# A two-layer block on one core: how the first layer's pool stage applies its modulation, and what the first expert weights wait for

## The reference, cut to what matters

```
sh1, sc1, g1, sh2, sc2, g2 = silu(c) @ w_mod[0] + b_mod[0]       # 6 x 1024, once for c and once for c_ctx
a = rmsnorm(x) * norm1_g * (1 + sc1) + sh1                        # per channel
mean_g = windowed mean over tokens of a (windows 2, 4, 8, 16, one per group of 256 channels)
y = ((mean_g - a) @ pool_w[g] + pool_b[g]) * pool_ls
x = x + g1 * y
h = rmsnorm(x) * norm2_g * (1 + sc2) + sh2
gates = top 2 of 16 experts in the best group, from h @ w_route   # hierarchical
x = x + g2 * sum_e gates[e] * (silu(h @ w_gate[e]) * (h @ w_up[e])) @ w_down[e]
```

## Time and profile before

| | |
|---|---|
| median of three runs | 2296.31 us |
| the profiled execution | 2297.54 us, of which span 2296.1 us |
| PE busy | 2149.3 us, 94% |
| DVE, ACT, POOL busy | 1295.4, 1033.7, 134.8 us |
| head and route, to the last store's landing | 0 to 137.4 us |
| first layer's experts | 142.7 to 322.7 us |
| DMA over the span | 324.17 MB, mean 141 GB/s |

### The profile page before, as it was taken

One profiled execution on the slowest core, in us unless ns is written; L12 is line 12 of the kernel. 1 busy time (PEld: TensorE's weight loads), 2 busy tenths in 40 slices (PEclk: granted clock), 3 DMA queues, 4 the chain that ended last, 5 costly groups with the idle time before them and its releaser, 6 DMA issues.

```text
span 2296.1 us, 31361 instructions
## 1 busy us (share of the span) xinstructions
PE 2149.3 (94%) x13248; PEld 1648.1 (72%) x13248; DVE 1295.4 (56%) x1837; ACT 1033.7 (45%) x1501; POOL 134.8 (6%) x112
## 2 busy tenths in 40 slices
PE   6879989999996998999889999998999998999997
PEld 4666654577774665777667888886877776888885
DVE  2467766666637775355526766535255546766533
ACT  3446632155535664377745433324333355433331
POOL 0011200000001220000001000003000002000000
PEclk9979999999997998999999999999999999999998
DMA  9889980022217995211012222121322112212210
GB/s 400 325 344 368 382 348 0 1 111 94 93 47 276 352 361 219 83 65 38 37 74 92 91 110 110 74 100 61 109 94 79 63 56 91 111 74 110 110 55 37
DMA packets 40574, 324.17 MB, mean 141 GB/s; under 512 B 7231, under 2 KB 8255, under 8 KB 21695
## 3 DMA queue, kind: packets, MB, share of 16 engines
q1 hardware_dynamic: 27288, 288.91, 32.6%
q0 software_dynamic: 10624, 25.71, 3.3%
q10 hardware_dynamic: 2512, 7.41, 0.8%
HBM read 310.40 MB, written 24.19 MB: 146 GB/s over the span
## 4 chain that ended last, share of the span: by engine, by line
PE 85%; DVE 6%; ACT 4%; DMA 3%; issue 1%; POOL 0%; SPq 0%; ACTq 0%; POOLq 0%; DVEq 0%
PE PS L163 79%; PE PS L911 2%; DMA work<-tokens,slots 1%; PE PS L661 1%; DVE work L2360 1%; ACT work L1606 1%; PE PS L1172 1%; DVE WR L2366 1%; DMA tokens<-work 0%; ACT XH L1304 0%; ACT work L1611 0%; ACT L1611 0%; DMA work<-ys 0%; DMA work<-in_xtok 0%; ACT work L1602 0%
## 5 line engine op out<-in xcount | busy, mean ns | idle before, releaser
L163 PE MATMUL PS<-HS,RS 128*128 128x512 f32 x4128 | 951.2, 391 | 9.4 <-DVE HS L2137 8.6
L163 PEld LDWEIGHTS PS<-HS,RS 128*128 128x128 f32 x4128 | 773.8, 188 | 175.5 <-issue 13.9
L1780 DVE TENSOR_TENSOR RS<-ring,RS 128x1024 fp32r<-128x1024 f32 x212 | 259.0, 1225 | 342.3 <-ACT RS L1268 342.3
L1268 ACT ACTIVATE RS<-ring 128x1024 fp32r<-128x1024 f32 x212 | 221.6, 1052 | 252.3 <-PE PS L163 252.3
L1703 ACT ACTIVATE work<-work,vec 128x512 f32<-128x512 f32 x88 | 72.0, 818 | 239.5 <-DVE work L2487 239.5
L1780 DVE TENSOR_TENSOR CR<-ring,WR 128x1024 fp32r<-128x1024 f32 x128 | 153.3, 1221 | 35.9 <-ACT WR L1268 33.2
L163 PE MATMUL PS<-work 128*64 128x128 f32 (+5 forms) x1728 | 131.2, 293 | 29.6 <-DVE work L1839 19.7
L1268 ACT ACTIVATE WR<-ring 128x1024 fp32r<-128x1024 f32 x128 | 134.8, 1058 | 50.7 <-PE PS L163 46.9
L163 PEld LDWEIGHTS PS<-work 128*64 128x64 f32 (+2 forms) x1728 | 106.9, 147 | 49.3 <-issue 30.9
L1268 ACT ACTIVATE work<-PS 128x384 f32<-128x384 f32 (+2 forms) x194 | 86.9, 484 | 115.8 <-PE PS L694 37.4
L163 PE MATMUL PS<-RS,HS 128*128 128x512 f32 x480 | 116.1, 400 | 8.3 <-DVE HS L2137 8.3
(11 more groups left out here) (258 smaller groups left out, 2804.8 us busy)
## 6 DMA issues: line engine op xcount, KB each, us to landing
ring<-in_wexp SPq DMA_DIRECT2D x32, 2048.0 KB, 11.1
ring<-in_wmod SPq DMA_DIRECT2D x24, 2048.0 KB, 10.2
ring<-in_ffnu SPq DMA_DIRECT2D x22, 2048.0 KB, 8.0
ring<-in_wexp SPq DMA_DIRECT2D x32, 1024.0 KB, 11.2
ring<-in_ffnd SPq DMA_DIRECT2D x10, 2048.0 KB, 7.3
ring<-in_dilqk SPq DMA_DIRECT2D x6, 2048.0 KB, 8.1
ring<-in_sbqk SPq DMA_DIRECT2D x4, 2048.0 KB, 8.1
ring<-in_dilv SPq DMA_DIRECT2D x3, 2048.0 KB, 8.0
```

Source lines behind the costliest of these rows:

```text
L163: return T.matmul(out, l, r, start=start, stop=stop, skip_group_check=True)
L1268: return S.activation(out, x, ACT.Copy, **kw)
L1780: V.tensor_tensor(lo, src, hi.bitcast(F32), ALU.subtract).then_inc(w_lo, 1)
```

## The change

The head applies the first modulation to the copied means instead of to the weights. DVE's `scaled_means(s)` multiplies the 8 chunks of a stream in place by `aff`; `shift_edges(s)` adds sh1 times the edge constants straight to the first and last 8 tokens of `HT` and signals `ad_aff`. So `shift_products` and `add_edges` go, one `poolw` serves both streams, `product(i)` waits for `ad_aff` 3 (latent) or 4 (context), and the ring's cell 8 is free. Because sh1 is needed before the products, modulation tiles 2 and 3 are turned ahead of them. On PE, `rows(6)` moves in front of the latent sums and the context sums stand behind `stat_spread(2)`. On ACT, the last four products stand between the first four squares. SP waits for all token stores before `wup` 0 and for the first gather before `wup` 1.

```diff
@@ the ring, and the products on PE
-    ring.over[8] = (pl_y, 17)
...
             def product(i):
                 s, c = i // 8, i % 8
-                g = c // 2
                 pe.wait_ge(*(means_copied(12 + i) if i < 4 else (md_b, i - 3)))
-                pe.wait_ge(md_a, 8 * s + 2 * g + 2)
+                pe.wait_ge(ld_work, 16)
+                pe.wait_ge(ad_aff, s + 3)
...
-            def shift_products():
...
@@ order on PE, from cols(1) on
+            rows(2)
+            rows(3)
+            cols(2)
+            cols(3)
             for i in range(4):
                 product(i)
...
@@ ACT
-            for i in range(16):
+            ada(2, 6)
+            ada(3, 7)
+            for i in range(12):
                 product(i)
-                if i % 4 == 3:
-                    ada(2 + i // 4, 6 + i // 4 % 2)
+                if i in (3, 7):
+                    ada(4 + i // 4, 6 + i // 4)
             for c in range(8):
                 square(2, c, XL[:, c, :], pl_x, c + 1)
+                if c < 4:
+                    product(12 + c)
+            ada(6, 6)
             root(2)
-            ada(6, 6)
+            ada(7, 7)
@@ DVE
-            def scaled_weights(s):
+            def scaled_means(s):
+                dve.wait_ge(pl_ma, 4 * s + 4)
+                dve.wait_ge(pl_md, 4 * s + 4)
                 for c in range(8):
-                    V.tensor_scalar(scaled_w[s][:, c // 2, c % 2, :], poolw[:, c // 2, c % 2, :], aff[:, 0, 0, c, s:s + 1],
-                                    None, ALU.mult).then_inc(md_a, 1)
+                    x = pool_rows(8 * s + c)
+                    V.tensor_scalar(x, x, aff[:, 0, 0, c, s:s + 1], None, ALU.mult).then_inc(md_a, 1)
...
+                dve.wait_ge(md_a, 8 * s + 8)
+                V.tensor_tensor(h[:, :, 0:8], h[:, :, 0:8], e[:, :, 0:8], ALU.add)
+                V.tensor_tensor(h[:, :, n - 8:n], h[:, :, n - 8:n], e[:, :, 8:16], ALU.add).then_inc(ad_aff, 1)
...
             ada(2, 6)
             ada(3, 7)
-            dve.wait_ge(pl_y, 13)
-            for s in range(2):
-                shift_edges(s)
-            add_edges(0)
+            dve.wait_ge(ad_mod, 4)
+            shift_edges(0)
+            scaled_means(1)
+            shift_edges(1)
@@ SP
         for n in range(6, 16):
             load("wmod", n)
+        sp.wait_ge(ht_out, 96)
         load("wup", 0)
+        sp.wait_ge(xg[0], 16)
         load("wup", 1)
```

More of the change, by code:

```diff
@@ L554, in pool_mix @@
             cols(1)
+            rows(2)
+            rows(3)
+            cols(2)
+            cols(3)
             for i in range(4):
                 product(i)
-            rows(2)
+            rows(4)
             product(4)
             product(5)
-            cols(2)
+            cols(4)
             product(6)
             product(7)
-            rows(3)
+            rows(5)
             product(8)
             product(9)
[L566 to L576, removed]
             cols(5)
+            for i in range(10, 16):
+                product(i)
+            rows(6)
             for c in range(8):
                 stat_add(2, c)
-            rows(6)
+            rows(7)
+            cols(6)
+            pe.wait_ge(md_b, 16)
+            stat_spread(2)
             for c in range(8):
                 stat_add(3, c)
[L583 to L587, removed]
             cols(7)
+            rows(8)
             stat_spread(3)
-            for U in (8, 9):
-                rows(U)
-                cols(U)
+            cols(8)
+            rows(9)
+            cols(9)
             rows(10)
@@ L1347, in pool_mix @@
             root(3)
-            for n in (7, 8, 9):
+            for n in (8, 9):
                 ada(n, 6 + n % 2)
@@ L1744, in act_program @@
         attention()
-        act.wait_ge(ad_aff, 10)
+        act.wait_ge(ad_aff, 12)
         shifted(3, 1, (0,), lambda c, s: HL[:, c, :])
@@ L1846, in means @@
                 V.tensor_copy(pool_rows(i), pool_bank(i)[:, 0:(512, 256)[i // 8]]).then_inc(pl_md, 1)
-            def scaled_weights(s):
+            def scaled_means(s):
+                dve.wait_ge(pl_ma, 4 * s + 4)
+                dve.wait_ge(pl_md, 4 * s + 4)
                 for c in range(8):
-                    V.tensor_scalar(scaled_w[s][:, c // 2, c % 2, :], poolw[:, c // 2, c % 2, :], aff[:, 0, 0, c, s:s + 1],
-                                    None, ALU.mult).then_inc(md_a, 1)
+                    x = pool_rows(8 * s + c)
+                    V.tensor_scalar(x, x, aff[:, 0, 0, c, s:s + 1], None, ALU.mult).then_inc(md_a, 1)
             def shift_edges(s):
-                q = PS[:, 1, 0:16].rearrange("p (g j s) -> p g j s", g=4, j=2)[:, :, :, s]
+                shift = mod[:, 0, 0:8, s].rearrange("p (g j) -> p g j", j=2)
                 r = C("edge").rearrange("p (g e) -> p g e", g=4)
-                step(V.tensor_tensor(edges[:, s, :, :, :], q.unsqueeze(3).to_broadcast([128, 4, 2, 16]),
+                step(V.tensor_tensor(edges[:, s, :, :, :], shift.unsqueeze(3).to_broadcast([128, 4, 2, 16]),
                                      r.unsqueeze(2).to_broadcast([128, 4, 2, 16]), ALU.mult))
-            def add_edges(s):
+                e = edges[:, s, :, :, :].rearrange("p g j e -> p (g j) e")
+                h = HT[:, :, 0:512] if s == 0 else HT[:, :, 512:768]
                 n = (512, 256)[s]
[L1863 to L1866, removed]
+                dve.wait_ge(md_a, 8 * s + 8)
+                V.tensor_tensor(h[:, :, 0:8], h[:, :, 0:8], e[:, :, 0:8], ALU.add)
+                V.tensor_tensor(h[:, :, n - 8:n], h[:, :, n - 8:n], e[:, :, 8:16], ALU.add).then_inc(ad_aff, 1)
             def add(s):
@@ L1879, in pool_mix @@
             ada(0, 6)
-            for i in (8, 10, 12):
+            for i in (8, 10, 12, 14):
                 means(i)
-            means(14)
             ada(1, 7)
@@ L1899, in pool_mix @@
             add(0)
-            add_edges(1)
             add(1)
@@ L2167, in attention @@
             rcp(5)
-            scaled(2, 0, (4, 5), lambda c, s: HT[:, c, 0:512] if s == 0 else HT[:, c, 512:768], 8)
+            scaled(2, 0, (4, 5), lambda c, s: HT[:, c, 0:512] if s == 0 else HT[:, c, 512:768], 10)
             step(V.tensor_scalar(a_qs, VC("qg"), 0.125, None, ALU.mult))
@@ L2525, in dve_program @@
         pool_mix()
-        scaled(1, 1, (2, 3), lambda c, s: HT[:, c, 0:512] if s == 0 else HT[:, c, 512:768], 6)
+        scaled(1, 1, (2, 3), lambda c, s: HT[:, c, 0:512] if s == 0 else HT[:, c, 512:768], 8)
         moe(0, 6, route(0, 6))
@@ L2530, in dve_program @@
         attention()
-        scaled(3, 1, (6,), lambda c, s: HL[:, c, :], 10)
+        scaled(3, 1, (6,), lambda c, s: HL[:, c, :], 12)
         moe(1, 4, route(1, 4))
```

25 lines of the change are left out of this document (7 added, 18 removed).

## The result

| | before | changed |
|---|---|---|
| median, all runs side by side | 2296.61 us (4 runs, 2294.18 to 2297.09) | 2284.14 us (4 runs, 2282.88 to 2285.29) |
| profiled execution | 2297.54 us, span 2296.1 | 2285.29 us, span 2283.8 |
| PE busy | 2149.3 us | 2138.7 us |

The ratio is 0.9949 with an interval of 0.9933 to 0.9965: faster by 0.5%. The forecast was 2285.0 us, from 2280 to 2292.3, with 0.87 on faster. Nearly all of the gain lies where the prediction put it. The first up product on PE starts 11.67 us earlier, the combination after the experts (PE's first step of it, at 309.5 instead of 320.5 us) 11.0 us earlier, and the profiled execution is 12.25 us shorter.

A forecast was written before the change was run, and what follows sets the result against it. PE, 94% busy, was taken to bound the kernel, with the head one serial chain. Shifts along it summed to 11.3 us at the first up product: profiled 2297.5 to 2286.2, median 2285.0 us, range 2280 to 2292.3.

The forecast's parts named there:

- The scaled means: On DVE in the head: eight chunks of 512 at 0.4 us each, 3.2 us in all, done at 41.5.
- The start of the products: On PE: the first product waits for sh1, scaled means and edges, and starts at 43.4, 4.3 us later.
- low-clock products: Rival in the head: tile 3 or edges late, products partly at low clock, 7 us lost, 2292.3 us; chance 0.07.
- The add: On DVE: `add(0)` waits for `cols(5)`, not for the products, and starts at 64.2, 10.6 us earlier.
- ACT's squares: On ACT: the fifth square waits for PE's sum behind `rows(6)`, so only 6.9 of the 10.6 us arrive.
- From the root to h: Statistics to h, with `rows(7)` at half clock: h starts at 87.5 instead of 98.33, 10.8 us gained.
- The store: Last token store, no longer beside `wup` loads: 3.6 us instead of 11.3, landed at 118.8, 18.6 us earlier.
- The load: `wup` 0, issued after the store: 8.7 us plus 1.3 for three gathers beside it, landed at 128.8.
- The hand-over: From the last store's issue at 115.2 to the first up product on PE at 136.4: 21.2 us.
- Later stages: After `up(0)`: the stages keep their lengths, so the shift there and at the end should be the same.
- PE's one wait for a gather: Sign of a wrong forecast: PE waits for gathers in the experts' part, where it was busy 119.8 of 122 us.
- the rival of a late stream: Rival in the experts' part: gathers land behind weight loads, 13 waits of 1 us, 2298.0 us; chance 0.05.

The follow-up runs named there:

- the repeat: The changed kernel run again without any edit, beside the kernel that holds modulation tile 5: 2280.82 us, ratio 0.9925.
- the variant of `rows(6)`: Changed kernel with PE's rows of modulation tile 6 moved from ahead of the latent sums to behind the fourth: 2281.72 us, ratio 0.9924.
- tile 4 held: Changed kernel with SP's load of modulation tile 4 and all after it held until PE has done tile 3's rows: 2284.06 us, ratio 0.9947.
- waits alone: The kernel before plus only SP's two new waits, ahead of `wup` 0 and `wup` 1: 2291.89 us, ratio 0.9982.
- tile 5 held: Changed kernel with SP's load of modulation tile 5 and all after it held until PE has done tile 3's rows: 2283.09 us, ratio 0.9936.
- free first load: Changed kernel without the wait for token stores before `wup` 0; `wup` 1 still waits for the first gather: 2283.84 us, ratio 0.9946.
- without the waits: Changed kernel with SP's two new waits, before `wup` 0 and `wup` 1, taken out again: 2285.46 us, ratio 0.9959.
- tile 5 held, first load free: Changed kernel with tile 5's load held until tile 3's rows are done and `wup` 0 not waiting for the stores: 2286.34 us, ratio 0.9953.

## Why the prediction was right, step by step

The sum was right within 1 us, by errors in both directions, so that it came this close is in part luck. (The root's forecast is its old time less the 6.9 us of the last sum.)

| at | before | forecast | measured |
|---|---|---|---|
| `cols(1)` done on PE | 37.8 | 37.8 | 38.6 |
| first product | 39.06 | 43.4 | 46.53 |
| `add(0)` on DVE | 74.74 | 64.2 | 68.62 |
| root of the latent sum | 81.63 | 74.7 | 78.19 |
| h | 98.33 | 87.5 | 89.38 |
| last store issued | 126.00 | 115.2 | 117.04 |
| last store landed | 137.3 | 118.8 | 119.68 |
| `wup` 0 landed | 127.2 | 128.8 | 128.45 |
| `up(0)` | 147.68 | 136.4 | 136.01 |
| profiled execution | 2297.54 | 2286.2 | 2285.29 |

- **The scaled means** cost 3.26 us for eight, 0.4 each, as taken between 0.4 and 0.54. Tile 3 was there: 59 of its 64 records ran without a wait. DVE's last edge step releases the first product (1.07 us), as forecast.
- **The start of the products** was mis-sized: 7.5 us later instead of 4.3. Of the missing 3.2 us, 2.1 are the stop inside `rows(3)`, which no term of the sum held, and 0.9 a later `cols(1)`, which the repeat does not have. (The forecast's own terms, 41.7, 0.6 and 0.8, give 43.1 and not 43.4.) The first 16 records at a low clock then take 1.5 us more than in the earlier trace rows. The prediction had weighed low-clock products as a rival, but for another reason, and at 7 us. The kernel before had one modulation tile between other work here; the changed one has two in a row, 64 short matmuls in 128 records.
- **The add** follows `cols(5)` (67.82 to 68.62) and not the last product (73.2), as forecast. It is 6.1 us earlier instead of 10.6, by the start above and the low clock.
- **ACT's squares** do wait for the sum behind `rows(6)`, 1.58 us, and the variant of `rows(6)` shows that this is worth 1.2 us at h. This step is shown. The first square, 1.6 us behind the add, is as forecast too (70.23 against 68.62).
- **From the root to h** the changed kernel takes 11.2 us. Forecast was 12.8, with `rows(7)` at half clock (3.64); it ran in 1.93 us at the full one. PE is busy 19.23 of the 20 us from 70 to 90. This gave back 1.7 us of the late start. In all, h came 8.95 us earlier instead of 10.8.
- **The store** alone took 2.64 us; 3.6, from the lone scatter, was too much. The repeat had 3.87, but there the store before it was in flight for 2.4 us of them. The term was bounded by 3.6 below, and that bound was wrong.
- **The load** took 8.75 us from its issue with three gathers beside it. The 1.3 us put on top of 8.7 for them were not needed in this execution. Elsewhere the same load took 7.6 (tile 4 held), 8.0 (waits alone), 8.9 (tile 5 held), 9.2 (repeat) and 10.1 us (`rows(6)` moved), so the 10.0 of the sum lies within its scatter. The gathers paid instead: the first landed near 129.4, 8 us after its issue, against 4.4 in the earlier trace rows; the split hid that. The Trainium skill ("DMA: Bandwidth & Descriptors", "Anatomy of one DMA") would have made it 6.8 us, an estimate by a formula that this section fits to transfers issued by GpSimd, while SP issues this one; the measured 8.75 decides. The advice that the prediction took from the same page stands in its "Rules for kernel authors", to issue a transfer early and wait for it late, and this trace agrees with it: the load that was held back is what ACT waits for (1.25 us).
- **The hand-over** was therefore 19.0 us instead of 21.2, and these 2.2 us (1.0 of the store, 1.2 of the load) covered the 1.9 that the head fell short.
- **Later stages** kept their lengths. 173.5 us from `up(0)` to the combination against 172.8, and 10.5 us for the first period in both; ACT's 2.08 us for `wup` 1 delay nothing that PE needs. The 0.7 us by which the first of these stretches grew is PE's one wait for a gather, which the prediction had named as a sign of being wrong; the repeat has no such wait and 172.9 us. So the rival of a late stream, 13 gathers at 1 us each, fell, but one gather in one of two profiles did come late.

So the sign and the mechanism were right: 8.8 us from the rework, 2.4 to 2.9 from the waits on top of it. What the waits do was understood only in part. The prediction put the store's fall from 11.3 to 3.6 us on `wup` 0 and 1 together. The free first load shows that `wup` 1 is the one that hurts: with `wup` 0 alone beside it the store takes 9.4 us but costs only 0.8, since tile 15's copy, at 127, is nearly as late, and the first load, already in, lets the split start 1.3 us earlier. In that light the wait on the stores is neutral here.

That the stop is late instructions is inferred, but tightly. It comes at one record of a dense run of short matmuls with nothing waited for, the same record in all seven profiles that have it (after 123 of 128), and it shrinks with the load on the DMA engines. An instruction queue (q8) carries single packets of 16 KB, each about 1 us long, and their times fit the stops. The DMA view of the changed kernel, 41.5 to 42 us:

```profile
q8 instruction: 1, 0.02, 12.7%
```

The table has the start of this packet in each kernel, beside PE's stop:

| kernel | packet starts | PE stops | PE goes on | from packet to going on |
|---|---|---|---|---|
| changed | 41.77 | 42.24 | 44.34 | 2.57 |
| changed, repeat | 40.84 | 41.37 | 43.47 | 2.63 |
| without the waits | 40.31 | 40.93 | 42.81 | 2.50 |
| first load free | 40.95 | 41.35 | 43.38 | 2.43 |
| `rows(6)` moved | 41.07 | 41.39 | 43.49 | 2.42 |
| tile 5 held, first load free | 39.72 | 41.29 | 42.20 | 2.48 |
| tile 5 held | 39.14 | 41.28 | 41.68 | 2.54 |
| tile 4 held | 38.91 | no stop | | |

PE goes on 2.4 to 2.6 us after the packet starts, however long it has stood. With tile 4 held the packet starts 3.3 us before PE reaches the place (42.2), and there is no stop. So the stop is as long as the packet is late, and the packet comes earlier when fewer loads run. The profile does not say which engine a packet is for; that is the step which stays inferred. All ten profiles, the kernel before too, have one or two more such stops between 76 and 101 us, of 0.42 to 2.01 us, inside or at the start of other runs of short matmuls and 2.2 to 2.7 us behind the start of such a packet. In the changed kernel that one (0.48 us at 91.88) is off the chain.

Open is why the clock fell after a gap of 0.40 us and 1.07 of waiting, but not, in the kernel with the empty queue, after 1.07 alone.

## What to carry to other kernels

Where a load is held back to free a transfer, hold the one whose user is far off, and check what else ends at the same time: here the second load was worth 3.3 us and the first nothing. A gain in a serial head is kept only as far as the next thing that is ready late; count those candidates (store, load, last modulation tile) before paying for an edit. A long run of short matmuls, with the DMA engines full, may leave PE without instructions for a while; where the profile names nothing for a stop, look for an instruction packet that started shortly before it. Whether longer work between the two tiles would hide the packet was not tried.

## What the runs showed of the hardware

- **PE without instructions.** Stops of 1.88 to 2.10 us in five profiles (the changed kernel twice, without waits, with the first load free, `rows(6)` moved), 0.91 and 0.40 with one tile fewer in the queue, none with the DMA engines idle; each ended 2.4 to 2.6 us after a 16 KB packet of the instruction queue had started. The Trainium skill ("Runtime: NRT & Kernel Launch", "Instruction fetch mechanics") says that instructions come in 16 KiB blocks over a DMA queue of their own and that this is mostly hidden, since instructions are issued more slowly than they are fetched. If these stops are that fetch, it was not hidden here.
- **A store beside loads.** 512 KB took 2.6 us with no load beside it in four profiles and 3.87 in a fifth (the repeat, behind another store), 7.5 to 9.4 us beside one 2 MB load (tile 15, or `wup` 0), and 11.3 to 13.5 beside two.
- **The clock on the route.** PE ran at 0.50 in 110 to 112 us in one variant and at 1.00 in the repeat, in the same work, and it cost 1.6 us up to the last store's issue. The same 1.6 us part two executions of one kernel, the changed one.
- **Scatter.** The same code from the combination to the end took 1971.9 to 1979.4 us in the profiled executions, more than the variants of the changed kernel differ at `up(0)` (134.6 to 138.9).
